# A two-layer trunk on one core: early loads of y, a pipelined last stage, and empty expert slots left out

## The reference, cut to what matters

```python
def hier_moe(x, norm_w, w_group, w_expert, w_gate, w_up, w_down):
    h = rmsnorm(x, norm_w)
    g_sel = argmax(h @ w_group)                      # one of 4 groups
    top_p, top_e = top_k(softmax(logits of that group's 8 experts), 2)
    weights = p_g * top_p / sum(top_p)
    # every token goes to 2 of 32 experts: 4096 assignments, in blocks of 128 rows of one expert
    yb = (silu(xb @ w_gate[e]) * (xb @ w_up[e])) @ w_down[e] * weight
    out = zeros.at[token].add(yb)                    # both experts of a token are added

def reference(x, ...):
    for layer in range(2):
        x = x + mixer(x, ...)                        # GLA in layer 0, RG-LRU in layer 1
        x = x + hier_moe(x, ...)
    return rmsnorm(x, final_norm)
```

## Time and profile before

| | |
|---|---|
| median of 3 runs | 3014.77 us |
| the profiled execution: its time, its span | 3014.33 us, 3012.6 us |
| TensorE matmul busy | 2619.9 us, 87% of the span |
| VectorE, ScalarE, GpSimd busy | 1820.9, 1647.7, 590.5 us |
| moved by DMA | 573.61 MB, mean 190 GB/s |
| gathers (L1327), scatters of y (L1347) | 194, 103 |

### The profile page before, as it was taken

How to read it: one execution, slowest core, us unless ns; L and a number is a source line. 1 busy time by engine, 2 the same in 40 slices (tenths; PEclk the granted TensorE clock), 3 DMA queues, 4 the chain that set the end, 5 groups by cost and what they waited for, 6 DMA issues and landing times. The chain is left out here.

```text
span 3012.6 us, 41660 instructions
## 1 busy us (share of the span) xinstructions
PE 2619.9 (87%) x12246; PEld 2100.4 (70%) x12246; DVE 1820.9 (60%) x3169; ACT 1647.7 (55%) x2260; POOL 590.5 (20%) x795
## 2 busy tenths in 40 slices
PE   6999999999799599999976999999599589999850
PEld 4878878788688477777755777777488467777640
DVE  4555555554456566565636888877465577556546
ACT  5565565554344366565635666675444376555532
POOL 0000000000011344555430000000011255545420
PEclk9999999999899799999987999999799799999985
DMA  3223223331445589789866545451444599877867
GB/s 122 90 91 101 89 91 105 104 107 57 142 155 167 173 295 312 273 281 323 271 218 215 175 166 168 144 171 63 128 154 147 178 350 337 289 264 265 307 237 293
DMA packets 388258, 573.61 MB, mean 190 GB/s; under 512 B 33408, under 2 KB 304000, under 8 KB 384000
## 3 DMA queue, kind: packets, MB, share of 16 engines
q1 hardware_dynamic: 353104, 457.23, 45.8%
q0 software_dynamic: 32688, 105.99, 9.4%
q10 hardware_dynamic: 2304, 8.39, 0.7%
HBM read 449.32 MB, written 122.22 MB: 190 GB/s over the span
## 5 line engine op out<-in xcount | busy, mean ns | idle before, releaser
L1445 DVE TENSOR_TENSOR experts_gu_lo<-carry_raw,experts_gu_hi 128x1024 fp32r<-128x1024 f32 x256 | 296.6, 1220 | 64.4 <-ACT experts_gu_hi L1404 62.4
L1327 POOL DMA_INDIRECT experts_rows<-h_rows,experts_source_now x194 | 269.8, 1391 | 274.0 <-PE experts_ps L1497 129.3
L118 PE MATMUL experts_ps<-experts_gu_hi,experts_hT_hi 128*128 128x512 f32 x760 | 316.3, 416 | 3.0 <-issue 3.0
L119 PE MATMUL experts_ps<-experts_gu_lo,experts_hT_hi 128*128 128x512 f32 x760 | 300.3, 395 | 0.0
L120 PE MATMUL experts_ps<-experts_gu_hi,experts_hT_lo 128*128 128x512 f32 x760 | 299.9, 395 | 0.0
L1404 ACT ACTIVATE experts_gu_hi<-carry_raw 128x1024 fp32r<-128x1024 f32 x256 | 250.2, 1057 | 52.5 <-DMA carry_raw<-in_moe_w_up 42.8
L1456 DVE TENSOR_TENSOR experts_hT_lo<-experts_ps,experts_hT_hi 128x512 fp32r<-128x512 f32 x194 | 133.2, 687 | 240.6 <-ACT experts_hT_hi L1383 233.6
L963 POOL MEMSET route_empty<- 128x512 int32 x2 | 1.1, 564 | 1322.1 <-POOLq L160 1322.1
L118 PE MATMUL route_ps<-route_w_hi,route_src_hi 128*128 128x512 f32 x512 | 208.6, 407 | 45.7 <-DVE route_src_lo L1029 45.7
L1396 ACT ACTIVATE experts_y<-experts_ps,experts_by_block 128x1024 f32<-128x1024 f32 x99 | 110.6, 1117 | 213.8 <-DMA y_rows<-experts_y,experts_target_now 208.4
L119 PE MATMUL route_ps<-route_w_lo,route_src_hi 128*128 128x512 f32 x512 | 203.4, 397 | 0.0
(11 more groups left out here) (322 smaller groups left out, 6757.1 us busy)
## 6 DMA issues: line engine op xcount, KB each, us to landing
carry_raw<-in_moe_w_gate SPq DMA_DIRECT2D x64, 1024.0 KB
carry_raw<-in_moe_w_up SPq DMA_DIRECT2D x64, 1024.0 KB
ahead_wd_raw<-in_moe_w_down SPq DMA_DIRECT2D x64, 1024.0 KB
gla_w_raw<-in_gla_w_in SPq DMA_DIRECT2D x32, 1024.0 KB, 7.3
ahead_wd_raw<-in_lru_w_in SPq DMA_DIRECT2D x32, 1024.0 KB
gla_w_raw<-in_gla_w_in SPq DMA_DIRECT2D x32, 512.0 KB, 5.1
route_src<-oT_rows SPq DMA_DIRECT2D x32, 512.0 KB
x_rows<-route_x_new SPq DMA_DIRECT2D x32, 512.0 KB, 2.9
```

Of the source, the lines that this page charges most:

```text
L118: nc.tensor.matmul(out, w_hi, x_hi, start=first, stop=False)
L119: nc.tensor.matmul(out, w_hi, x_lo, start=False, stop=False)
L1327: pool.indirect_dma_start(rows[:, b], None, h_halves[b], bass.IndirectOffsetOnAxis(source_now[b][:].bitcast(U32), 0))\
L1445: nc.vector.tensor_tensor(gu_lo[:, slot(e), of_part(c)], gu_raw[:, slot(e), of_part(c)], gu_hi[:, slot(e), of_part(c)].bitcast(F32), ALU.s ...
```

## The change

1. *Early y.* A hook `when_stored` runs on SP when GpSimd has seen the last scatter land: a new semaphore `all_stored` is raised behind GpSimd's last wait. In layer 0 it loads the first tile of y for `lru`, in layer 1 the first four tiles of y for `finish`, into the memory that held w_gate and w_up (`carry`). These loads now stand ahead of the border.
2. *The last stage.* Every tile of x has a buffer of its own, y has nine buffers, h eight (before: six, four, four). DVE adds up tile t+1 before it scales tile t; ScalarE stores tile t-1 after the root of tile t.
3. *Table.* In `lru` and `finish` a first, unused `Sqrt` stands ahead of the first tile.
4. *Empty slots.* The source row is no longer cut to 11 bits, so an empty slot's is 2048 or more. The gather has `bounds_check=T - 1, oob_is_err=False` and the scatter `bounds_check=2 * T - 1, oob_is_err=False`: entries over the bound are left out. `rows` is set to zero once at the start of each expert stage, by GpSimd.
5. `LruEarly` is created behind `project_and_route` rather than ahead of it, which only moves it in memory.

```diff
--- experts
+        all_stored = m.plain("all_stored")
@@ SP
             after_all(sp, lambda: sp.wait_ge(wd_lo_done, nth(E - 1)))
+            sp.wait_ge(all_stored, 1)
+            when_stored(sp)
@@ GpSimd
             pool.memset(y[:], 0.0)
+            pool.memset(rows[:], 0.0)
...
                 pool.indirect_dma_start(rows[:, b], None, h_halves[b],
-                                        bass.IndirectOffsetOnAxis(source_now[b][:].bitcast(U32), 0))\
+                                        bass.IndirectOffsetOnAxis(source_now[b][:].bitcast(U32), 0),
+                                        bounds_check=T - 1, oob_is_err=False)\
...
                 pool.indirect_dma_start(y_rows, bass.IndirectOffsetOnAxis(target_now[:].bitcast(U32), 0),
-                                        y[:], None).then_inc(y_stored, DMA)
+                                        y[:], None, bounds_check=2 * T - 1, oob_is_err=False).then_inc(y_stored, DMA)
...
             pool.wait_ge(y_stored, nth_stored(blocks + 1))
             stand(pool)
+            pool.sem_inc(all_stored, 1)
@@ VectorE
-                nc.vector.tensor_scalar(sources[:, columns], lists[:, columns, 0], 1, T - 1,
-                                        ALU.logical_shift_right, ALU.bitwise_and).then_inc(sources_set, 1)
+                nc.vector.tensor_scalar(sources[:, columns], lists[:, columns, 0], 1, None,
+                                        ALU.logical_shift_right).then_inc(sources_set, 1)
--- LruEarly, FinishEarly
+    def load_y(self, sp, y_rows):
+        sp.dma_start(self.y_ab[:], y_rows[0:2 * P, :].rearrange("(p c) d -> p c d", c=2)).then_inc(self.y_in, DMA)
...
+    def load_y(self, sp, y_rows):
+        for t in range(self.Y_TILES):
+            sp.dma_start(self.y[:, t], y_rows[2 * t * P:2 * (t + 1) * P, :].rearrange("(p c) d -> p c d", c=2))\
+                .then_inc(self.y_in[t], DMA)
--- lru
-            for t in range(2):
-                load_y(t)
+            load_y(1)
...
+            nc.scalar.activation(warm[:], k.eps[:], ACT.Sqrt)
             mean_square(0)
--- finish
-    DEPTH, XD = 4, FinishEarly.TILES
+    DEPTH, XD, YE, YD = 8, FinishEarly.TILES, FinishEarly.Y_TILES, 9
...
@@ SP
+            for t in range(YE, NT):
+                if t >= XD:
+                    sp.dma_start(x[t], x_dram[t * P:(t + 1) * P, :]).then_inc(x_in[t], DMA)
+                after(sp, x_done, t - YD)
+                sp.dma_start(y_ab[t % YD], y_tiles[t]).then_inc(y_in[t % YD], DMA)
@@ ScalarE
+            nc.scalar.activation(warm[:], k.eps[:], ACT.Sqrt)
...
-                after(act, h_done, t)
-                act.dma_start(out[t * P:(t + 1) * P, :], h[:, j]).then_inc(stored[j], DMA)
+                if t:
+                    store(t - 1)
+            store(NT - 1)
@@ VectorE
+            combine(0)
             for t in range(NT):
                 j = t % DEPTH
-                dve.wait_ge(early.x_in[t % XD], (t // XD + 1) * DMA)
-                dve.wait_ge(y_in[j], (t // DEPTH + 1) * DMA)
-                step(nc.vector.tensor_tensor(x[:, t % XD], x[:, t % XD], y_ab[:, j, 0], ALU.add))
-                nc.vector.tensor_tensor(x[:, t % XD], x[:, t % XD], y_ab[:, j, 1], ALU.add).then_inc(x_done, 1)
+                if t + 1 < NT:
+                    combine(t + 1)
                 after(dve, std_done, t)
```

More of the change, by code:

```diff
@@ L1672, in lru @@
         x_in = early.x_in
-        y_in = [m.plain(f"y_in{j}") for j in range(2)]
+        y_in = [early.y_in, m.plain("y_in1")]
         x_stored = [m.plain(f"x_stored{j}") for j in range(2)]
@@ L2069, in _, with store @@
         def _(sp):
-            for t in range(NT):
-                after(sp, x_done, t - DEPTH)
-                sp.dma_start(y_ab[:, t % DEPTH], y_tiles[t]).then_inc(y_in[t % DEPTH], DMA)
-                late = t + XD - DEPTH
-                if t >= DEPTH and late < NT:
-                    after(sp, h_done, late - XD)
-                    sp.dma_start(x[:, late % XD], x_dram[late * P:(late + 1) * P, :])\
-                        .then_inc(early.x_in[late % XD], DMA)
+            for t in range(YE, NT):
[3 more added lines that the diff above has]
+                sp.dma_start(y_ab[t % YD], y_tiles[t]).then_inc(y_in[t % YD], DMA)
         @block.scalar
         def _(act):
+            def store(t):
+                after(act, h_done, t)
+                act.dma_start(out[t * P:(t + 1) * P, :], h[:, t % DEPTH]).then_inc(stored[t % DEPTH], DMA)
+            nc.scalar.activation(warm[:], k.eps[:], ACT.Sqrt)
             for t in range(NT):
```

48 lines of the change are left out of this document (32 added, 16 removed).

## The result

| | before | changed |
|---|---|---|
| median of 4 runs each | 3014.51 us | 2982.35 us |
| lowest to highest | 3010.44 to 3019.16 | 2978.58 to 2987.29 |
| the profiled execution: time, span | 3014.33, 3012.6 us | 2987.29, 2985.6 us |
| moved by DMA | 573.61 MB | 536.91 MB |

A forecast was written before the change was run, and what follows sets the result against it. In the last stage one tile's chain and the DMAs were taken as nearly equal bounds; TensorE was busy through most of the expert loops. Gains of 17.2 + 5.5 + 5 = 27.7 us from 3014.3 gave 2987 us, range 2967 to 3001.

The forecast's parts named there:

- last stage: Last stage: earlier y and a shorter chain leave the DMAs as the bound at 400 GB/s; gain 17.2 us.
- start of the recurrent stage: Start of `lru`: y load 4.2 us earlier and table load hidden, 1.3 us; gain 5.5 us.
- empty slots: Expert loops: a third of the slots are empty, skipping their bytes gains 5 us, at most 34.
- The shorter chain: Last stage: one tile's chain (5.48 us) and its DMAs are nearly equal, so shortening it meets the DMA bound at once.
- my own formula: Last stage: 29.4 MB over the DMA rate, from 1 us after the first y load's issue, gives the last y's landing.
- Load ahead of the border: Start of `lru`: the first y load goes out before the border, data just behind it; gain 4.2 us.
- the table load out of the gap: Start of `lru`: the 1.28 us table load between square and root moves into the wait for y; gain 1.3 us.
- the fullest DMA engine keeps its load: Expert loops: empty slots end each block, so engines serving the first slots stay as busy; skip gain taken as 5 us.
- rival of the slower issue: Expert loops: bounds checks lengthen GpSimd issues, loss 120 times the extra; at 0.5 us each, 3052 us; chance 0.10.
- rival of a large skip: Expert loops: skipping empty slots gains 20 us or more instead of 5, time 2972 us; chance 0.20.
- last stage at 372 GB/s: Last stage: rate stays at its second half's and the skip gives nothing, 2997 us; chance 0.20 shared with late loads.
- late loads: Early y loads: GpSimd's release no sooner than the border, 3.5 and 4.2 us lost, 2995 us; chance 0.20 shared with slow rate.

The follow-up runs named there:

- e1: Kernel before with only the bounded gathers and scatters, uncut source rows and zeroed rows: 3011.67 us, ratio 0.9981.
- e4: Whole change without the skip of empty slots (no bounds, sources cut to 11 bits, no zeroing of rows): 2991.22 us, ratio 0.9912 to the kernel before.
- e11: Same file as e4, the whole change without the skip of empty slots, on another chip: 2989.04 us, ratio 0.9909 to the kernel before.
- e6: Whole change, but the last stage adds tile t only after scaling tile t-1 and stores it behind its own root: 3001.02 us, ratio 0.9943.
- e7: Whole change with the old buffer counts in the last stage (y 4, x 6, h 4): 2980.94 us, ratio 0.9882 to the kernel before.
- e2: Kernel before with only the early loads of y for both stages: 3009.49 us, ratio 0.9977.
- e5: Whole change with bounds checked but no entry out of bounds, so all bytes move: 2996.75 us, ratio 0.9934 to the kernel before.
- e12: Same kernel as e5, bounds checked but nothing out of them, on the chip of e11: 2998.61 us, ratio 0.9941 to the kernel before.
- e8: Whole change plus eight more x tiles loaded during the last experts, first two y tiles into w_down's memory: 2971.58 us, ratio 0.9850 to the kernel before.

## Why the prediction was right, point by point

I forecast 2987 us from a sum of 27.7 us; measured were 2982.35 us and 32.2 us. The three terms against what the runs gave:

| term | forecast (bounds) | measured |
|---|---|---|
| last stage | 17.2 (11.7 to 20.9) | 20.6 (profile) |
| start of the recurrent stage | 5.5 (3 to 5.5) | 6.6 (profile), 0.8 of it by the skip |
| empty slots | 5 (0 to 34) | 4.5 to 5.7 (e1, e4, e11) |
| sum | 27.7 | 31 to 32, the 0.8 counted once; whole time 32.2 |

**Last stage: right mechanism, size off by 3.4 us.** The shorter chain did run into the DMAs at once, DVE began to wait for y at the ninth tile (2940.73 us in the timeline), and e6 and e7 show that the new order, not the buffers, removed the old bound. The mis-sized term is the rate. I took 400 GB/s as a mean between loads alone (421) and the mixed second half (372), although the 394 and 372 GB/s of the earlier trace rows were both taken while the chain, not the queues, asked for 383. A rate at a share near 1 was read as what the DMAs can do; it was what they were asked for, and the share doesn't tell: it read 0.98 to 1.01 at 372 to 394 GB/s and reads 1.02 at 425. With 425 GB/s my own formula gives 29.4 MB / 425 = 69.2 us and a last y at 2905.7 + 69.2 = 2974.9; it was added from 2975.69. The rate alone would have added 73.5 - 69.2 = 4.3 us to the gain, and the load that goes out a little sooner some tenths more; the last addition, 0.8 us later than my formula has it, and the tail of 9.9 us rather than 9.2 took part of it back. From the last landing to the end I had forecast 84 us; it is 81.

The Trainium skill, "DMA: Bandwidth & Descriptors", section Bandwidth, has about 358 GB/s as the limit between HBM and SBUF, and in its table of a single core's loads 425 GB/s for 16 MB with the pair's other core idle. The trace agrees with the table and not with the 358: 423 to 425 GB/s over 40 us of loads and stores in both directions.

**Recurrent stage: 6.6 instead of 5.5 us**, above the upper bound that I had given. Load ahead of the border (4.6 us in e2, forecast 4.2) and the table load out of the gap (12.8 in e2 against 11.6 us in e4 and e11: 1.2, forecast 1.3) are as the steps had it. I had assumed that the load goes out 2.8 us after the scatter's issue ended; without the skip it is 2.43, which is the 0.4 us between 4.6 and 4.2. The 0.8 us above that come from a step I had left out: with the skip the last scatter moves 0.02 MB instead of 0.52, and the load goes out after 1.61 us. Without the skip the stretch is 11.6 us long, with it 10.8.

**Empty slots: the net was right, its reason was not.** I had reckoned with a gain near nothing, since the fullest DMA engine keeps its load, and with a check that costs nothing, since an issue's time doesn't depend on its rows. Both halves were wrong and cancelled, so that the net of 5 us came out right is luck. Leaving out the bytes brings 12 to 14 us (e5, e12 against the whole change). The check costs 7 to 10 us (e5 against e4, e12 against e11). The rival of the slower issue was priced at 120 times its extra time. With 0.086 us for each gather and 0.058 us for a scatter, 0.077 us on average, that is 9 us, near what e5 and e12 measured. So it fits that its mechanism was real and only its size small, though the waits of e11 and e12 are all that shows it at work; it stayed well short of the 0.19 us from which it would have taken all the gain. The rival of a large skip is excluded by e1 as a net gain: 20 us would be a ratio of 0.9934. That TensorE's share rose by 0.6 and 1.1 points, as forecast by less than 2, agrees.

The Trainium skill, "DMA: Bandwidth & Descriptors", section The descriptor swizzle, has each DMA engine serve fixed partitions. I had drawn from it that the skip would be worth nothing in most blocks of one expert. The 12 to 14 us of the bytes speak against that conclusion; which engines the skipped rows relieve stays open, since no run here shows the engines apart.

**The other two rivals.** A last stage at 372 GB/s is excluded by 425; late loads by the issue at 2904.71, 3.8 us ahead of the border's end. My bound that the border could be up to 0.7 us later for DVE was not needed: the border took 6.1 us (6.2 without the skip) as against 6.3, with SP's 2.08 us of issues inside it.

**Hidden costs taken as nothing.** The zeroing of `rows` is hidden, as I had it. From the first IOTA of the first expert stage to the table load on ScalarE it takes 4.47 us before and 4.46 us in the changed kernel. GpSimd, which does the zeroing, waits 2.15 us instead of 2.94 for the source rows and issues its first gather 6.07 instead of 5.89 us after that IOTA; in e12, also with the zeroing, it is 5.88. The shorter source rows and the place of `LruEarly` had no run of their own; the loop of layer 0 scatters by 7 us, so a cost of theirs below that is not excluded by it.

## What to carry to other kernels

When a chain of engines and the DMAs take almost the same time per tile, the rate read there is the chain's demand, not the DMAs' limit; take the limit from a stretch in which loads queue up, and size the stage behind the edit with it. Once a stage is bound by bytes, move bytes to a stretch with idle queues: e8 took 10.5 us out of the last stage by that alone, while more buffers in the bound stage brought nothing. And an option on an instruction that is issued hundreds of times needs a run of its own with the option on and its effect off: here it showed a gain of 12 to 14 us and a cost of 7 to 10 behind a net of 5.

## What the runs showed of the hardware that I had not expected

- Loads and stores together ran at 423 to 425 GB/s over 40 us, no slower than the 421 of loads alone before, which was read over only 3 us.
- An indirect transfer with a bounds check takes a MOVE of 29 ns ahead of it and a longer issue on GpSimd. For the gathers the shortest issue is 966 to 969 ns in the five profiles without a check and 1023 in the eight with a check and all of w_up; the medians are 999 to 1043 and 1056 to 1092 ns (1092 in the changed kernel). For the scatters the medians are 995 to 998 and 1024 ns.
- A scatter takes 144 packets whether it moves 0.52 MB or 0.02. Entries out of bounds save bytes, not packets: the software queue has 32688 packets in both kernels, with 105.99 and 69.29 MB, and 8944 more packets are under 512 bytes. The bytes fit to 3968 empty slots of 8 KB (32.5 MB) and eight further scatters of 0.52 MB whose rows are all out of bounds (4.2 MB).
- The loop of layer 0 differs by up to 7 us between profiles of kernels with the same expert stage (545.2 to 551.9 us with the skip), more than the skip brings. Of an effect of 5 us a single pair of profiles shows nothing.
